# Expert rows gathered four to a token: column-quarter sums for groups of four rows in a ring of eight

## The chip, the core and the metric

The kernel runs on one core of one Trainium2 chip. The metric is device time in microseconds (us) of one execution. PE is TensorE, DVE VectorE, ACT ScalarE, POOL GpSimd, SP the queue that issues the weight transfers. Everything is float32; a float32 matmul stands in the trace as two MATMUL instructions and two weight loads, so "x8" is four matmuls.

## The reference, cut to what matters

Two transformer-like blocks over 256 tokens of 1024 numbers. The change is in one layer of the first block, a mixture of 16384 tiny experts of which each token uses 128:

```python
def peer(h, w_query, sub_keys, expert_u, expert_v):
    ...                                  # two top-16 searches for each of 8 heads
    eidx = ...                           # (tokens, 128) expert numbers
    gate = softmax(top_s)                # (tokens, 128)
    u = expert_u[et]                     # a row of 1024 for every token and expert
    v = expert_v[et]
    act = gelu(einsum('tnd,td->tn', u, xt)) * gt
    return einsum('tn,tnd->td', act, v)
```

Beside it stands work that does not depend on it: the second block's scan over 256 context tokens (projections, a solve by doubling in 64x64 pieces, a chain of states) and a small projection.

## The kernel before

The tokens are two blocks (b = 0, 1) of 128, one token to a partition. `u` and `v` lie side by side in `experts`, so one gather (`pool_rows`, line 1187) fetches 128 rows of 2048 numbers, 1 MB: row i of a tile is the i-th expert of each of the 128 tokens. There are 256 gathers, into a ring of `RING = 9` slots, three groups of `GROUP = 3`. POOL issues a gather into a slot once the slot's former row was used.

For each group, in order: DVE multiplies each row's `u` half with the tokens in `normed` and sums (`dve_group`, line 1197), ACT takes the gelu (1213), DVE multiplies by the gate (1201), ACT builds a 128x128 diagonal matrix of the results for each row (1219), and PE multiplies it with the `v` half, 2 x 512 columns, and so adds up all rows in PSUM (`pe_group`, 1231). From group 26 on (`WIDE`) the third row of each group does not go to PE: DVE adds it to `xres` (1208). At the end of a block `dve_rows_out` (1264) adds the PSUM sums to `xres`.

The order of everything around it is written out by hand in `run_order` (2185). A "turn" is one group; after each group every engine does the next "piece" of the work beside it from the list `pieces`: first the expert searches of the seven later quarters (`dve_select`, five pieces for each, spread over 24 turns), then the context block: its norm, 7 pieces of projection (`pe_ctx_in`), 2 of `dve_scan_common`, and for each of two directions 5 pieces of `pe_direction`/`dve_direction` and two pairs of 9 pieces of the solve (`pe_pair`), then 4 pieces of chain and the projection: 85 pieces in 86 turns. PE does piece n after group n, while ACT and DVE do it after group n+1 (`lag`). Every engine's queue is strictly in this order, so a piece that waits holds up the engine's next group. The search of the first quarter (b = 0) runs alone, before the first gather.

`AUX[:, 0:2, :]` (`SUMS`) collects the rows; the searches take their scores from `sc`, copied out of PSUM by ACT in `act_queries`.

## Time and profile before

| | us |
|---|---|
| median of 3 runs | 1682.56 (1682.3 to 1685.46) |
| the profiled execution | 1685.36 |
| its span | 1683.8 |
| PE busy | 1394.0 (83%) |
| DVE busy | 1029.3 (61%) |
| ACT busy | 358.7 (21%) |
| POOL busy | 347.3 (21%) |
| moved by DMA | 406.98 MB, of which 297.35 MB by the software queue of the gathers |

The profile cuts the span into 40 slices of 42.1 us; a digit is the busy share in tenths. The gathers run in slices 8 to 25. PEclk is the clock that the throttle granted TensorE, as a share of 2.4 GHz. "Idle before, releaser" tells what ended an engine's idle time. Times of day below are us from the start of the span.

### The profile page before, as it was taken

Reading aid. Unit: us, or ns where it says so; the run is one execution under the profiler, and the core shown is the slowest. Engines: PE = TensorE matmul, PEld = TensorE weight load, DVE = VectorE, ACT = ScalarE, POOL = GpSimd, SP = SyncE. Lnnn points to the kernel's source line nnn. Section 1 sums busy time; section 2 is a strip of 40 time slices with the busy share of each in tenths; the row PEclk is TensorE's granted clock in tenths of the full one; section 3 lists DMA queues with packets and bytes.
Section 4 is the critical chain, followed back from the end, with each engine's and each line's share of the span. In section 5 each row is a group of like instructions: output and inputs, shape, how many; then the busy total and the mean of one; then the engine's idle time right before and its main releaser. Section 6 shows DMA issues by size and latency. Waiting matters only on the chain.

```text
span 1683.8 us, 24922 instructions
## 1 busy us (share of the span) xinstructions
PE 1394.0 (83%) x10614; PEld 940.2 (56%) x10614; DVE 1029.3 (61%) x2175; ACT 358.7 (21%) x696; POOL 347.3 (21%) x315
## 2 busy tenths in 40 slices
PE   7989898957677797588859897779987878899997
PEld 6468764832233264255525554347877763788843
DVE  2967765539999877868788777421554343355511
ACT  3012400112222322421242121212342210111100
POOL 1000011124344444445545454000000000000000
PEclk9988998979887898899988998789999999899998
DMA  9453387599989999799999999524200021344442
GB/s 373 165 176 116 110 323 259 187 324 420 373 323 383 366 356 407 267 391 416 419 376 365 418 417 415 219 75 150 101 8 3 4 103 50 112 151 154 154 159 83
DMA packets 110735, 406.98 MB, mean 242 GB/s; under 512 B 10376, under 2 KB 35472, under 8 KB 77344
## 3 DMA queue, kind: packets, MB, share of 16 engines
q0 software_dynamic: 44576, 297.35, 44.3%
q1 hardware_dynamic: 62720, 104.36, 18.1%
q10 hardware_dynamic: 3328, 3.68, 1.2%
q8 instruction: 83, 1.36, 0.3%
q14 instruction: 28, 0.23, 0.0%
HBM read 404.30 MB, written 1.07 MB: 241 GB/s over the span
## 4 chain that ended last, share of the span: by engine, by line
PE 58%; DVE 23%; DMA 8%; ACT 5%; issue 4%; POOL 1%; ACTq 0%; DVEq 0%; another core or an unknown queue 0%
PE psum L489 24%; DVE arena L1197 9%; PE psum L499 7%; PE psum L1231 6%; PE psum L1582 6%; DMA arena<-in_experts,arena 6%; PE psum L2038 4%; PE psum L1785 2%; DMA weights<-in_w_in 1%; PE psum L585 1%; DVE arena L1156 1%; DVE arena L1157 1%; DVE arena L1154 1%; PE psum L708 1%; PE psum L1926 1%
## 5 line engine op out<-in xcount | busy, mean ns | idle before, releaser
L1231 PE MATMUL psum<-arena 128*128 128x512 f32 x792 | 405.9, 665 | 142.0 <-ACT arena L1219 141.6
L489 PE MATMUL psum<-actT,weights 128*128 128x256 f32 x1824 | 404.0, 384 | 5.3 <-ACT actT L602 2.3
L1187 POOL DMA_INDIRECT arena<-in_experts,arena x256 | 317.5, 1240 | 437.9 <-PE psum L1231 370.5
L489 PEld LDWEIGHTS psum<-actT,weights 128*128 128x128 f32 x1824 | 351.1, 193 | 57.5 <-ACT actT L602 5.6
L1231 PEld LDWEIGHTS psum<-arena 128*128 128x128 f32 x792 | 161.8, 212 | 348.7 <-issue 200.3
L1197 DVE CUSTOM_DVE_ANT_0 arena<-normed,arena 128x1024 f32<-128x1024 f32 x256 | 304.7, 1223 | 61.1 <-DMA arena<-in_experts,arena 57.0
L1213 ACT ACTIVATE arena<-arena 128x3 f32<-128x3 f32 (+1 forms) x86 | 17.6, 204 | 441.0 <-DVE arena L1197 384.2
L1582 PE MATMUL psum<-arena 64*64 64x64 f32 (+1 forms) x2816 | 84.6, 224 | 17.5 <-DVE arena L1699 7.1
L1582 PEld LDWEIGHTS psum<-arena 64*64 64x64 f32 x2816 | 79.3, 135 | 24.5 <-issue 14.9
L499 PE MATMUL psum<-weights,actT 128*128 128x512 f32 x192 | 83.1, 593 | 2.1 <-DMA weights<-in_w_in 1.0
L944 POOL DMA_DIRECT2D arena<-in_ada_wT x48 | 25.3, 528 | 252.0 <-DVE mod L960 252.0
L1208 DVE SCALAR_TENSOR_TENSOR xres<-arena,xres 128x1024 f32<-128x1024 f32 x58 | 74.5, 1285 | 2.5 <-DVE arena L1201 0.6
L2038 PE MATMUL psum<-weights,arena 128*128 128x512 f32 x176 | 75.7, 593 | 0.0
L1219 ACT ACTIVATE arena<-const,arena 128x128 f32<-128x128 f32 x198 | 67.2, 393 | 19.8 <-DVE arena L1201 18.9
L499 PEld LDWEIGHTS psum<-weights,actT 128*128 128x128 f32 x192 | 36.3, 190 | 47.8 <-issue 44.9
L2082 DVE SCALAR_TENSOR_TENSOR arena<-arena,small 128x256 f32<-128x256 f32 x154 | 61.9, 480 | 0.0
L2038 PEld LDWEIGHTS psum<-weights,arena 128*128 128x128 f32 x176 | 33.5, 190 | 41.6 <-issue 41.5
L1582 PEld LDWEIGHTS psum<-actT,arena 64*64 64x64 f32 x1152 | 38.8, 134 | 17.5 <-issue 17.0
L2080 DVE TENSOR_SCALAR arena<-arena,small 128x256 f32<-128x256 f32 x22 | 6.8, 351 | 67.5 <-ACT arena L2055 67.5
L819 DVE SCALAR_TENSOR_TENSOR arena<-arena,small 128x256 f32<-128x256 f32 x120 | 47.6, 482 | 0.0
L1582 PE MATMUL psum<-actT,arena 64*64 64x64 f32 x1152 | 44.5, 221 | 3.6 <-issue 3.4
L544 ACT ACTIVATE normed<-xres 128x1024 f32<-128x1024 f32 x7 | 7.4, 1056 | 173.3 <-DVE xres L2100 68.3
(347 smaller groups left out, 1537.4 us busy)
## 6 DMA issues: line engine op xcount, KB each, us to landing
weights<-in_w_in SPq DMA_DIRECT2D x18, 2048.0 KB, 8.9
arena<-in_ada_wT POOLq DMA_DIRECT2D x48, 512.0 KB, 5.8
weights<-in_ffn_w_up SPq DMA_DIRECT2D x22, 1024.0 KB, 6.8
weights<-in_ffn_w_down SPq DMA_DIRECT2D x5, 2048.0 KB, 7.9
weights<-in_w_out SPq DMA_DIRECT2D x4, 2048.0 KB, 15.0
weights<-in_w_peer_q SPq DMA_DIRECT2D x4, 2048.0 KB, 8.5
arena<-in_experts,arena POOLq DMA_INDIRECT x256
weights<-in_w_ple_gate SPq DMA_DIRECT2D x2, 2048.0 KB, 8.2
```

What stands on the lines that cost most here:

```text
L489: mm = nc.tensor.matmul(out[:, c * T:(c + 1) * T], w[:, k, c * P:(c + 1) * P], act[:, k, :], start=(k == 0), stop=(k == kc - 1))
L499: mm = nc.tensor.matmul(out[:, b * 512:(b + 1) * 512], act[:, k, b * P:(b + 1) * P], w[:, k, :], start=(k == 0), stop=(k == kc - 1))
L819: st.run(nc.vector.scalar_tensor_tensor(ycv[:, c, :], src, w, ycv[:, c, :], ALU.mult, ALU.add))
L1187: nc.gpsimd.indirect_dma_start(out=rows[:, n % RING, :], out_offset=None, in_=dram["experts"], in_offset=bass.IndirectOffsetOnAxis(ap=eidx ...
L1197: ins = nc.vector.tensor_tensor_reduce(rows[:, pos, 0:D], normed[:, b, :], rows[:, pos, 0:D], 1.0, 0.0, ALU.mult, ALU.add, dots[:, g, j:j ...
L1208: nc.vector.scalar_tensor_tensor(xres[:, b, :], rows[:, pos, D:2 * D], acts[:, g, ON_PE:GROUP], xres[:, b, :], ALU.mult, ALU.add).then_inc ...
L1219: nc.scalar.activation(diag[:, pos, :], K("ident"), ACT.Copy, scale=acts[:, g, j:j + 1]).then_inc(S("diag_ok"), 1)
L1231: mm = nc.tensor.matmul(SUMS[:, i, :], diag[:, pos, :], rows[:, pos, D + 512 * i:D + 512 * (i + 1)], start=first, stop=last, skip_group_ch ...
L1582: mm = nc.tensor.matmul(dst[half[c], g, at + q * n:at + (q + 1) * n], left(g, c, q), right(g, c, q), start=True, stop=True)
L1785: mm = nc.tensor.matmul(out[:, c * T:(c + 1) * T], w[:, k, c * P:(c + 1) * P], actT[:, k, :], start=(k == 0), stop=(k == DC - 1))
L2038: mm = nc.tensor.matmul(aux[2 * b + n], ffT[:, f, b * P:(b + 1) * P], w[:, k, 512 * n:512 * (n + 1)], start=(f == 0), stop=(f == FC - 1))
L2082: st.run(nc.vector.scalar_tensor_tensor(dst, src, w, dst, ALU.mult, ALU.add))
```

## The change

The 128 slots of a gather are dealt differently: a tile holds for 32 tokens (a quarter of the block) four rows each. Of the 32 gathers of one search, number i serves token quarter g = i % 4, and its partition 32 j + m holds expert 8 j + i // 4 of token 32 g + m; so four gathers in a row serve the four token quarters. Bytes and number of gathers are the same. So the dots need the tokens of a quarter on all four partition quarters (`quad_tokens`, written to DRAM and read back four times), and numbers and gates must be moved from the partition of their token to the four quarters: DVE multiplies them by a mask `quad`, PE sums with `ident_q`, DVE copies out of PSUM. The stationary matrix of a row is now 128x32, and its sum goes to 32 partitions of PSUM; the four rows of a group take the four column quarters of the array.

`RING` is 8 and `GROUP` 4: two groups. All rows go to PE; DVE's addition at 1208 and its gate multiplication at 1201 are gone, and ACT multiplies by the gate, one instruction for each row. PE waits for all four matrices of a group. The pieces are cut anew (ten for each search, a search begun every 8 pieces, 119 in all) and taken two to a turn: 60 of the 64 turns have pieces. PE's first projection of the context waits for all searches.

```diff
-RING = 9
-GROUP = 3
+RING = 8
+GROUP = 4
+QUADS, QP = 4, 32
...
+        high = r.take(2 * D).rearrange("p (g n) -> p g n", g=2)
+        quad_tokens = (normed, high)
...
+        SPREAD = {what: PS[:, 2 * (tile_at["ctx_k"] % 2) + i, 0:HEADS * PK] for i, what in enumerate("eg")}
+        FIRST_E = AUX[:, 0, 0:HEADS * PK]
+        def pe_spread(pe, what, turn, dst):
+            pe.wait_ge(S(f"spread_{what}_in"), turn + 1)
+            if turn:
+                pe.wait_ge(S("eidx_ok" if what == "e" else "gates_done"), turn)
...
+            for j in range(QUADS):
+                mm = nc.tensor.matmul(dst[QP * j:QP * (j + 1), :], K("ident_q"), src[:, n * j:n * (j + 1)],
+                                      start=True, stop=True)
+        def act_quad_tokens(act, b, half):
+            for j in range(QUADS):
+                src = normed_rows[b * P:(b + 1) * P].rearrange("(g t) d -> t g d", g=QUADS)
+                act.dma_start(quad_tokens[half][QP * j:QP * (j + 1), :, :], src[:, 2 * half:2 * half + 2, :]).then_inc(
+                    S(f"quad_in{half}"), 16)
         def pe_queries(pe):
...
             for i in range(QUARTERS + 1):
+                if i == QUARTERS - 1:
+                    pe_spread(pe, "e", 0, FIRST_E)
...
+                    if i == QUARTERS - 1:
+                        pe_spread(pe, "g", 0, SPREAD["g"])
+                        pe.wait_ge(S("eidx_ok"), 1)
...
+            act.dma_start(normed_rows.rearrange("(b p) d -> p b d", p=P), normed).then_inc(S("normed_out"), 16)
...
         def dve_group(dve, b, t, g, count):
             for k, pos, n, filled in turn_slots(b, t, g * GROUP, count):
+                half = k % QUADS // 2
+                if isinstance(t, int) and t == 0 and k < QUADS and k % 2 == 0:
+                    dve.wait_ge(S(f"quad_in{half}"), 16 * QUADS * (b + 1))
                 dve.wait_ge(S(f"row{pos}"), filled * 16)
...
-            dve.wait_ge(S("gelu_ok"), t * PER_TURN + (GROUPS * b + g + 1))
-            nc.vector.tensor_tensor(acts[:, g, 0:count], gelu[:, g, 0:count],
-                                    gate[:, b, bass.ds(t * RING + g * GROUP, count)], ALU.mult).then_inc(S("acts_ok"), 1)
-            if count == GROUP and not wide(b, t, g):
...
-                nc.vector.scalar_tensor_tensor(xres[:, b, :], rows[:, pos, D:2 * D], acts[:, g, ON_PE:GROUP],
-                                               xres[:, b, :], ALU.mult, ALU.add).then_inc(S("row_added"), 1)
         def act_group(act, b, t, g, count):
...
+            act.wait_ge(S("gelu_ok"), t * PER_TURN + (GROUPS * b + g + 1))
+            for j in range(count):
+                nc.scalar.activation(acts[:, g, j:j + 1], gelu[:, g, j:j + 1], ACT.Copy,
+                                     scale=gate[:, b, bass.ds(t * RING + (g * GROUP + j), 1)]).then_inc(S("acts_ok"), 1)
             for k, pos, n, filled in turn_slots(b, t, g * GROUP, count):
                 j = k - g * GROUP
...
+                act.wait_ge(S("acts_ok"), rows_ahead(b, t, g) + j + 1)
+                nc.scalar.activation(diag[:, pos, :], K("ident_q"), ACT.Copy,
+                                     scale=acts[:, g, j:j + 1]).then_inc(S("diag_ok"), 1)
+            if b + 1 < TB and isinstance(t, int) and t == TURNS - 1 and g == PER_TURN - 1:
+                for half in range(2):
+                    act_quad_tokens(act, b + 1, half)
         def pe_group(pe, b, t, g, count):
...
+            pe.wait_ge(S("diag_ok"), rows_ahead(b, t, g) + count)
+            for i in range(2):
+                for k, pos, n, filled in turn_slots(b, t, g * GROUP, count):
+                    part = slice(QP * (k % QUADS), QP * (k % QUADS + 1))
...
+                    mm = nc.tensor.matmul(SUMS[part, i, :], diag[:, pos, :], rows[:, pos, D + 512 * i:D + 512 * (i + 1)],
                                           start=first, stop=last, skip_group_check=True)
+                    if i:
+                        mm.then_inc(S("row_used"), 1)
...
         def pe_ctx_in(pe):
+            pe.wait_ge(S("eidx_ok"), QUARTERS * TB)
+            pe.wait_ge(S("gates_done"), QUARTERS * TB)
...
+        pieces = [sum(pieces[i:i + 2], []) for i in range(0, len(pieces), 2)]
```

In `dve_select` the gate's subtraction goes ahead of the two heads' index sums, which become a piece each; behind them stand the mask products, and in the last piece the copies of numbers and gates out of PSUM.

## Rows read from the trace of the kernel before

**Rows 1.** The page's 40 slices: granted clock and DMA share.
```profile
PEclk9988998979887898899988998789999999899998
DMA  9453387599989999799999999524200021344442
```
**Rows 2.** Stretches of the gathers: us, busy of PE, PEld, DVE, ACT, POOL (instructions), PEclk, DMA share, GB/s.
```profile
378.00:590.00 212.00, 151.19 (x289) 61.55 (x288) 195.37 (x701) 53.17 (x123) 87.60 (x73) 0.85 0.93 373
...
650.00:710.00 60.00, 32.58 (x91) 15.49 (x90) 52.56 (x63) 23.30 (x40) 24.32 (x18) 0.80 0.83 330
710.00:850.00 140.00, 123.38 (x1571) 74.16 (x1569) 106.86 (x172) 31.18 (x84) 69.38 (x57) 0.98 0.99 402
850.00:900.00 50.00, 30.52 (x163) 15.80 (x166) 42.18 (x55) 19.68 (x37) 20.39 (x15) 0.76 0.87 345
900.00:1061.00 161.00, 138.22 (x1605) 81.46 (x1597) 124.37 (x207) 32.10 (x91) 74.97 (x62) 0.93 1.00 412
```
**Rows 3.** The page's costliest groups: those of the row loop, and the solve's.
```profile
L1231 PE MATMUL psum<-arena 128*128 128x512 f32 x792 | 405.9, 665 | 142.0 <-ACT arena L1219 141.6
...
L1197 DVE CUSTOM_DVE_ANT_0 arena<-normed,arena 128x1024 f32<-128x1024 f32 x256 | 304.7, 1223 | 61.1 <-DMA arena<-in_experts,arena 57.0
L1213 ACT ACTIVATE arena<-arena 128x3 f32<-128x3 f32 (+1 forms) x86 | 17.6, 204 | 441.0 <-DVE arena L1197 384.2
L1582 PE MATMUL psum<-arena 64*64 64x64 f32 (+1 forms) x2816 | 84.6, 224 | 17.5 <-DVE arena L1699 7.1
...
L1208 DVE SCALAR_TENSOR_TENSOR xres<-arena,xres 128x1024 f32<-128x1024 f32 x58 | 74.5, 1285 | 2.5 <-DVE arena L1201 0.6
...
L1219 ACT ACTIVATE arena<-const,arena 128x128 f32<-128x128 f32 x198 | 67.2, 393 | 19.8 <-DVE arena L1201 18.9
```
**Rows 4.** Timeline of DVE in the solve: start, us, instruction [idle before <-releaser].
```profile
828.73 1.23 DVE L1197 CUSTOM_DVE_ANT_0 arena<-normed,arena 128x1024 f32<-128x1024 f32 x1 [1.26 <-DMA arena<-in_experts,arena]
```
**Rows 5.** Timeline of POOL and DVE: a group's first gather, its first and last dot.
```profile
623.10 1.17 POOL L1187 DMA_INDIRECT arena<-in_experts,arena  x1 [4.54 <-PE psum L1231]
...
631.29 1.23 DVE L1197 CUSTOM_DVE_ANT_0 arena<-normed,arena 128x1024 f32<-128x1024 f32 x1 [0.67 <-DMA arena<-in_experts,arena]
...
636.43 1.23 DVE L1197 CUSTOM_DVE_ANT_0 arena<-normed,arena 128x1024 f32<-128x1024 f32 x1 [1.41 <-DMA arena<-in_experts,arena]
```
**Rows 6.** Timeline of PE: full width, two column halves, four 64x64 tiles, one cold sum.
```profile
314.55 1.95 PE L1029 MATMUL psum<-arena 128*128 128x128 f32 x16
...
185.22 1.58 PE L699 MATMUL psum<-arena 128*64 128x128 f32 x16 [1.68 <-ACT arena L787]
...
715.54 0.92 PE L1582 MATMUL psum<-arena 64*64 64x64 f32 x46
...
830.88 5.40 PE L1231 MATMUL psum<-arena 128*128 128x512 f32 x8 [2.69 <-ACT arena L1219]
```
**Rows 7.** Timeline at the start: first gather, ACT's last load, first reused slot.
```profile
332.26 1.01 POOL L1187 DMA_INDIRECT arena<-in_experts,arena  x1 [35.49 <-DVE arena L1159]
...
361.36 4.21 ACTq L525 DMA_DIRECT2D arena<-in_ctx  x1
...
371.67 0.94 POOL L1187 DMA_INDIRECT arena<-in_experts,arena  x1 [28.35 <-PE psum L1231]
```
**Rows 8.** Timeline of DVE: the first search's first instruction, its last before the gathers.
```profile
316.38 0.88 DVE L1100 MAX8 arena<-arena 128x8 f32<-128x128 f32 x4 [13.00 <-ACT arena L1046]
...
331.80 0.18 DVE L1159 CAST arena<-arena 128x32 uint32<-128x32 f32 x1
```
**Rows 9.** Timelines of PE and DVE in the context block's projection, common part and direction.
```profile
641.10 5.34 PE L1785 MATMUL psum<-actT,weights 128*128 128x256 f32 x24
...
659.45 6.55 DVE L1430 RECIPROCAL actT<-actT 128x1024 f32<-128x1024 f32 x1 [1.71 <-ACT actT L1417]
...
701.16 2.74 PE L1469 MATMUL psum<-const,arena 128*128 128x128 f32 x16 [4.27 <-DVEq L1560]
```
**Rows 10.** Timeline of DVE: the last block's sums are added.
```profile
1081.66 1.22 DVE L1264 TENSOR_TENSOR xres<-xres,psum 128x1024 f32<-128x1024 f32 x1 [14.50 <-PE psum L1231]
```

More of the change, by code:

```diff
@@ L308, in build @@
         gate = r.take(TB * NSEL).rearrange("p (b n) -> p b n", b=TB)
-        dots = r.take(12).rearrange("p (g n) -> p g n", g=3)
-        gelu = r.take(12).rearrange("p (g n) -> p g n", g=3)
-        acts = r.take(12).rearrange("p (g n) -> p g n", g=3)
-        diag = r.take(RING * P).rearrange("p (g n) -> p g n", g=RING)
+        dots, gelu, acts = [r.take(RING).rearrange("p (g n) -> p g n", n=GROUP) for _ in range(3)]
+        diag = r.take(RING * QP).rearrange("p (g n) -> p g n", g=RING)
         rows = r.take(RING * 2 * D).rearrange("p (g n) -> p g n", g=RING)
+        high = r.take(2 * D).rearrange("p (g n) -> p g n", g=2)
+        quad_tokens = (normed, high)
         after_rows = r.at
@@ L341, in build @@
         gsum = r.take(HEADS)
+        spread_e, spread_g = [r.take(HEADS * PK * QUADS) for _ in range(2)]
         assert r.at <= ARENA - 3072
@@ L1110, in dve_select @@
             st.settle()
+            yield
             for g in range(n_s):
@@ L1182, in pool_rows @@
                     g, j = divmod(k, GROUP)
-                    if j == ON_PE and not wide(former[0], t, g):
-                        pool.wait_ge(S("row_added"), dve_added(former[0], t, g) + 1)
-                    else:
-                        pool.wait_ge(S("row_used"), pe_summed(former[0], t, g) + j + 1)
+                    pool.wait_ge(S("row_used"), rows_ahead(former[0], t, g) + j + 1)
                 nc.gpsimd.indirect_dma_start(
@@ L1238, in groups_of_rows @@
                 t, g = divmod(first, PER_TURN)
-                if t == TURNS:
-                    group(eng, b, t, 0, REST)
-                    first += 1
-                elif g or t == 0 or last - first < 2 * PER_TURN:
+                if g or t == 0 or last - first < 2 * PER_TURN:
                     group(eng, b, t, g, GROUP)
@@ L1245, in groups_of_rows @@
                 else:
-                    end = min(last // PER_TURN, TURNS)
-                    assert GROUPS * b + first >= WIDE
+                    end = min(last // PER_TURN, TURNS - 1)
+                    if group is act_group:
+                        eng.wait_ge(S("gates_done"), TB * QUARTERS)
                     with eng.Fori(t, end) as i:
@@ L1421, in dve_scan_common @@
             wait_freed(dve, m.tiles[0])
+            if not m.full:
+                product(dve, "ctx_lora")
             for c in range(RC):
@@ L2146, in build @@
         beside = [select_stage(b, q) for b in range(TB) for q in range(QUARTERS) if b or q]
-        at_select = [[(i, k)] if k != 2 else [(i, 2), (i, 3)]
-                     for i, f in enumerate(beside) for k in range(f["pieces"]) if k != 3]
         n_first = len(beside)
+        pieces = [[] for _ in range(SELECT_EVERY * (n_first - 1) + SELECT_PIECES)]
+        for i, f in enumerate(beside):
+            for k in range(f["pieces"]):
+                pieces[SELECT_EVERY * i + k].append((i, k))
         beside += [dict(act=act_ctx_norm, dve=dve_ctx_norm, pieces=1),
```

110 lines of the change are left out of this document (59 added, 51 removed).

## The prediction

> **What bounds the kernel now.** I read the slices first [rows 1]: from slice 8 to 25 the DMA share stands at 9 nearly throughout, and nowhere else. This is the stretch of the 256 gathers, and the only one that the change touches. Then the stretches [rows 2]. From 710 to 850 and from 900 to 1061 the DMA share is 0.99 and 1.00 at 402 to 412 GB/s, with DVE busy 76% and PE 86 to 88%: the gathers' bytes are the bound. A tile of 1.049 MB takes 2.55 us there, and the dots wait for it [rows 4]. In the searches (378 to 590) DVE is busy 195.37 of 212 us and DMA has 0.93: DVE is the bound, by a little. In 650 to 710 (DMA 0.83, DVE 52.56 of 60 us) and 850 to 900 (0.87, 42.18 of 50) DVE's lumps of the scan are.
>
> So PE's 405.9 us and DVE's 74.5 us in the row loop [rows 3] are mostly beside the transfers. What is to be had is the time in which DMA is not full: by 1 minus its share, 15 us in the searches, 10 in 650 to 710, 7 in 850 to 900, 3 elsewhere; some 35 us, with 12 us more around 372, where the ring has run dry.
>
> **What the change does to each engine.** PE: a group of four rows was 16 instructions of 0.43 us (405.9 us over 792 is 0.51 with the cold ones) one after another, 6.9 us; in four independent columns of four instructions it is 4 x 0.43 plus 0.2 to drain, 1.9 us, or 3.6 us at 1.2 GHz. That columns do run side by side I read from the trace [rows 6]: 16 instructions of 128 columns at full width took 1.95 us, while 16 on two column halves with the same 128 rows took 1.58, and 46 on four 64x64 tiles 0.92 us, 20 ns each, though each is 0.22 us long. The Trainium skill speaks against this (TensorE: Matmul & The Clock Gate, Part 3, What overlaps and what doesn't): weight loads overlap running matmuls only where the row group differs, and here all four columns use all rows. By it 16 loads, at its P/1.2 ns some 27 ns each, would stand bare, 0.4 us a group. The trace does not bear it out: the halves of L699 share their row groups and overlap all the same.
>
> DVE: loses 58 additions, 74.5 us, and 86 gate products of 0.16; gains, for each search, two mask products and two copies, each bounded by 0.18 [rows 8] and 1.0 us below, I take 0.2 to 0.3, so 0.8 a search and 7 us in all. ACT, for a group of four: gelu 0.20, four gate products, four matrices of 128x32. A product is bounded by 0.14 and 0.20 (gelu of 3 numbers [rows 3]), a matrix by 0.20 and 0.34 (67.2 us over 198, at 128 wide); nearer the lower ends as the tiles are small, so 0.2 + 0.7 + 0.85 and 0.2 for waits on itself: 2.0 us, where a row's first matrix was ready after 0.9. POOL: same 256 issues.
>
> **The new limit: a ring of two groups.** A slot's round is: issue of its gather, landing of the whole group, dots, ACT, sums, next issue. With two groups, a turn (four rows) can't be shorter than half a round. Before, there were three groups, and rows were given back one by one. The round's first part I take from a group whose first gather found the queue nearly empty: issued 623.10, first dot 631.29, third 636.43 [rows 5]; 13.3 us for three, with a fourth transfer 15.9. A row was still ahead in that queue, and weights moved beside it, so this is an upper end; the lower is four transfers (10.2) plus half of what the first dot shows beyond its own transfer (5.6), 13.0. I take 14.6. Then last dot 1.2, ACT 2.0, sums, and an estimated 0.3 us until POOL issues.
>
> In the searches PE does nothing but sums (2 to 4 of 10 us), so its clock will be low, as it is near 0.8 in 650 to 710 with PE busy half the time [rows 2]: 3.6 us. Round 21.7, turn 10.8 us against 10.2 of transfer. DVE's turn is below that: four dots 4.8 (304.7 over 256) and, of a search of 15.6 us [rows 8] plus 0.8, on average a quarter, 4.1 with the gate: 9 us, the worst pair near 10.5.
>
> In the solve (17 of the 31 later turns with pieces) the pairing bites. PE takes pieces 2n and 2n+1 before the next group's sums; 2n+1 needs what ACT and DVE make of 2n, and these do it only after the dots of that next group. So the sums come after dots, ACT's group 2.0, its copies 1.0, PE's piece 2.5: 5.7 instead of 2.0 after the dots (the piece: some 80 instructions at 84.6 us over 2816 [rows 3], 0.03 each; the copies: two of 512 columns, an estimate from 0.34 for 128). Round 14.6 + 1.2 + 5.7 + 1.9 + 0.3 = 23.7, turn 11.8 warm; PE idles 4 us in each such turn, and after 2.69 us of idleness 8 sums took 5.40 us instead of 3.6 [rows 6]. I take 11.8.
>
> **The sum**, from the first reused slot on, against the profiled execution:
> - Start. The first indices pass PE once more: +1.2 us on the first gather at 332.26. Eight rows land instead of nine. ACT is held by its loads until 361.36 + 4.21 [rows 7]; both come 2 us later since PE stands in the new mask sums. Then table, gelu, ACT and a cold sum: the first reused slot is issued at 374.3 instead of 371.67. It must wait for other small transfers, as before (DMA share was full there), so the third group's dots end at about 393.4.
> - 27 more turns in the searches at 10.8: 292, so 685.
> - 34 turns at 10.2: 347, so 1032.
> - Context norm: the sums of that group stand behind transposes that wait for the norm, +5. Projection: two pieces of 5.34 [rows 9] and sums, 12.5 us a turn for three turns, +6. Tokens of block 1: ACT issues eight loads, a landing takes up to 8 us (row 5's 8.2), DVE waits, +5. Together 16.
> - Common part and first direction: six pieces of DVE. The stretch 650 to 710 had DVE busy 52.56; without six additions of 1.28 and twenty dots of 1.19 some 21 us are left, with waits on ACT (7.4 us of idleness) 29; before it one more piece of 4.5. In three turns with 14 us of dots that is 48 for 31 of transfer; two slots' slack of 4 gone: +13. In one of them the sums stand behind PE's wait for DVE L1560 (idle 4.27 [rows 9]) and the preparation of 7 us, +7: together 20.
> - Second direction: the same without the common part, +10.
> - Solve: 17 turns, 11.8 instead of 10.2: +27.
> - Chain: two turns, serial between PE and DVE, +3.
> - After the last dot: ACT 2.0, sums 3.6 cold, semaphores: 6.5 to the end of the addition.
>
> 685 + 347 + 16 + 20 + 10 + 27 + 3 + 6.5 = 1114.5. Before, the addition ended at 1081.66 + 1.22 = 1082.9 [rows 10]. So +31.6 us. What follows is unchanged. The profiled execution took 1685.36, which is the upper end of the three runs; laid on the median 1682.56 it gives **1714 us**.
>
> **Rivals.** (1) The transfers stay the bound: ACT and sums are short enough that a round is below 20.4, and DVE, rid of 74.5 us, catches up. Then 61 turns of 10.2 from 393.4 (1016), half of the lumps (30), 6.5: 1052, which is 31 us less: **1652 us**. For it speak DVE's load and the dry ring at 372 that is no worse; against it that a round of 20.4 leaves 4.6 us between the last dot and the next issue even with 14.6 before it, and the pairing in the solve. Chance 0.2. (2) Half-way: searches at 10.4, solve at 10.8: 11 + 17 us less than the forecast, **1686 us**; chance 0.14. (3) The forecast, with everything from 1695 to 1755: 0.56. (4) The columns don't run side by side with 512 columns moving: 6.9 us warm or up to 13.8 cold for the sums, at least 5 more in a round, 2.5 in each of 61 turns: +150, **1865 us**. Against it [rows 6]; 0.04. By the skill's rule on weight loads alone it would be 0.4 a round, +12: 1726, inside the forecast. (5) Lumps and cold clock are worse (solve at 13.5, searches at 11.3: +29 + 14): 1757 and more, 0.06.
>
> The forecast and (1) part at a round of 20.4 us, in the searches and in the solve.
>
> Range for 8 in 10: down into rival (1), 1655, up to 1757. A measurement of this kernel can tell 0.2%, 3.4 us: faster than 1679.2 has rival (1) and a part of (2), 0.25; within, 0.06; slower the rest, 0.69.
>
> **What would show it.** PE's line of the sums: 1024 instructions with busy time near 110 to 220 us, not 440 or more (rival 4). DVE 70 us less busy. In the searches DMA share near 0.94 with DVE's dots idle before DMA, and POOL idle before PE; a group's turn 10.8 us. In the solve turns of 11.8 and a DMA share of 0.87; at 1.00 rival (1) is right. PEclk lower than now in slices 9 to 16. The last addition near 1114. Wrong I'd be above all if a group's landing is much shorter than 14.6 us once the queue runs empty each time, or if the new waits on ACT's own results cost more than 0.2.

## The result, and the profile of the changed kernel

The changed kernel takes 1800.41 us (median of 4 runs, 1797.06 to 1811.26), the kernel before 1682.52 beside it: 1.0707 times as long, 95% interval 1.0660 to 1.0755. That is +118 us. The forecast was +31.6 us and 1714, with a range up to 1757, which is 43 us below the result. So the direction was right and the size was not, by nearly a factor of four.

The 40 slices of the changed kernel's page, granted clock and DMA share, to be laid beside [rows 1] (a slice is 45.0 us here and 42.1 there; both count from 0):
```profile
PEclk9979998955656555876786778759999998899999
DMA  9444496999999999776887698952420002355432
```
Slices 9 to 15 look no worse than before in DMA share, a 9 throughout; the loss is plain to see only from slice 16 on. This first impression is wrong, as the stretches show (us, busy time of PE, PEld, DVE, ACT and POOL with their instructions, PEclk, DMA share, GB/s), cut at the ends of the groups 2, 29, 33, 37, 46, 49 and 58 of four rows:
```profile
392.00:699.00 307.00, 98.03 (x544) 19.02 (x544) 239.77 (x775) 71.15 (x265) 128.82 (x108) 0.58 0.96 369
699.00:765.00 66.00, 36.90 (x178) 23.67 (x179) 24.22 (x41) 15.47 (x47) 13.54 (x14) 0.71 0.83 280
765.00:839.00 74.00, 30.44 (x164) 18.84 (x162) 45.48 (x53) 27.16 (x65) 20.56 (x19) 0.70 0.64 244
839.00:956.00 117.00, 80.83 (x1552) 61.02 (x1552) 55.84 (x94) 31.25 (x106) 45.48 (x38) 0.79 0.84 327
956.00:1007.00 51.00, 19.99 (x184) 11.21 (x184) 31.29 (x41) 21.57 (x51) 14.11 (x11) 0.64 0.61 231
1007.00:1122.00 115.00, 78.58 (x1460) 57.72 (x1456) 56.37 (x94) 30.77 (x106) 41.83 (x37) 0.82 0.85 329
1122.00:1202.00 80.00, 34.18 (x240) 13.37 (x240) 32.20 (x61) 13.34 (x56) 19.74 (x19) 0.66 0.84 336
```
In the first stretch, the searches, the share is 0.96 and yet only 369 GB/s are moved. Before, 0.99 and 1.00 went with 402 to 412 GB/s [rows 2]. A DMA engine that is "busy" here moves less than it did there. The searches of before, where VectorE was the bound, moved no more, 373 GB/s at 0.93 [rows 2]. So in this stretch nothing is lost against before; what is missing is the gain that the relieved VectorE should have brought. The last dot of the 120th row ends at 698.7 us, before at 711.0, though before had by then done the context's projection and the common part [rows 9], and the changed kernel neither. The loss of the whole falls behind that row. In the two solve stretches (839 to 956, 1007 to 1122) the share is 0.84 and 0.85, where 0.87 was forecast and before had 0.99 and 1.00; PE is busy 69% of them and DVE 48%, so nothing in them is full.

The costliest groups of the row loop and the solve on the page, beside [rows 3] (busy us, mean ns of one | idle time of the engine just before them and what ended most of it):
```profile
L1275 PE MATMUL psum<-arena 128*32 128x512 f32 x1024 | 192.0, 890 | 313.7 <-ACT arena L1262 313.7
L1233 POOL DMA_INDIRECT arena<-in_experts,arena x256 | 299.2, 1169 | 573.8 <-PE psum L1275 476.1
...
L1246 DVE CUSTOM_DVE_ANT_0 arena<-arena 128x1024 f32<-128x1024 f32 x128 | 155.4, 1224 | 116.5 <-DMA arena<-in_experts,arena 106.5
L1246 DVE CUSTOM_DVE_ANT_0 arena<-normed,arena 128x1024 f32<-128x1024 f32 x128 | 153.2, 1223 | 70.3 <-DMA arena<-in_experts,arena 57.8
L1252 ACT ACTIVATE arena<-arena 128x4 f32<-128x4 f32 x64 | 13.1, 205 | 528.2 <-DVE arena L1246 510.0
L1626 PE MATMUL psum<-arena 64*64 64x64 f32 (+1 forms) x2816 | 87.1, 230 | 23.1 <-DVE arena L1743 7.1
...
L1262 ACT ACTIVATE arena<-const,arena 128x32 f32<-128x32 f32 x256 | 60.2, 305 | 0.0
...
L1257 ACT ACTIVATE arena<-arena 128x1 f32<-128x1 f32 x256 | 54.4, 283 | 5.9
```
The change does to the engines what it says. The sums keep PE busy for 192.0 us instead of 405.9, although each single instruction is longer (890 ns against 665): four run at a time. The additions on DVE are gone (DVE is busy 950.5 us, before 1029.3). But the dots now wait 106.5 + 57.8 = 164 us for gathers, before 57.0, and POOL waits 476 us for the sums that free its slots, before 370.5. Two engines were relieved that were not the bound, and the bound, the transfers, is fed late.

One round of a slot in the searches, out of the timeline of POOL, DVE, ACT and PE (start, us, instruction [idle before <-releaser]): group 17 from its first gather to the gather that takes its first slot again.
```profile
545.27 1.62 POOL L1233 DMA_INDIRECT arena<-in_experts,arena  x1 [3.93 <-PE psum L1275]
...
549.88 0.94 POOL L1233 DMA_INDIRECT arena<-in_experts,arena  x1 [0.31 <-issue]
...
560.96 1.22 DVE L1246 CUSTOM_DVE_ANT_0 arena<-arena 128x1024 f32<-128x1024 f32 x1 [1.26 <-DMA arena<-in_experts,arena]
562.22 0.20 ACT L1252 ACTIVATE arena<-arena 128x4 f32<-128x4 f32 x1 [8.94 <-DVE arena L1246]
562.52 0.85 ACT L1257 ACTIVATE arena<-arena 128x1 f32<-128x1 f32 x4
563.28 0.94 ACT L1262 ACTIVATE arena<-const,arena 128x32 f32<-128x32 f32 x4
564.27 3.64 PE L1275 MATMUL psum<-arena 128*32 128x512 f32 x16 [7.59 <-ACT arena L1262]
568.16 0.94 POOL L1233 DMA_INDIRECT arena<-in_experts,arena  x1 [5.17 <-PE psum L1275]
```
From 545.27 to 562.18, the end of the last dot, are 16.9 us; ACT takes 2.0, the sums 3.6, and 0.25 later the slot is issued again: 22.9 us. Over the 25 groups from 4 to 28 the means are 16.7, 2.0, 3.6 and 0.3, a round of 22.7 and a turn of 11.4. The forecast was 15.8, 2.0, 3.6, 0.3 and 10.8.

One turn of the solve, with a pair of pieces, from the timeline of all engines:
```profile
1068.75 1.21 DVE L1246 CUSTOM_DVE_ANT_0 arena<-arena 128x1024 f32<-128x1024 f32 x1
...
1070.00 0.20 ACT L1252 ACTIVATE arena<-arena 128x4 f32<-128x4 f32 x1 [8.47 <-DVE arena L1246]
1070.30 0.85 ACT L1257 ACTIVATE arena<-arena 128x1 f32<-128x1 f32 x4
1071.05 0.94 ACT L1262 ACTIVATE arena<-const,arena 128x32 f32<-128x32 f32 x4
...
1072.84 0.58 ACT L1711 COPY arena<-psum 128x512 f32<-128x512 f32 x1
1073.47 1.97 PE L1626 MATMUL psum<-actT,arena 64*64 64x64 f32 x32 [3.44 <-ACT arena L1711]
1075.23 1.92 PE L1626 MATMUL psum<-arena,actT 64*64 64x64 f32 x32
...
1076.94 1.69 PE L1626 MATMUL psum<-actT,arena 64*64 64x64 f32 x32
1078.56 1.92 PE L1275 MATMUL psum<-arena 128*32 128x512 f32 x16
1078.71 0.69 DVE L1743 TENSOR_TENSOR actT<-actT,psum 128x512 f32<-128x512 f32 x1 [8.75 <-PE psum L1626]
```
The matrices are ready at 1071.99, and the sums start at 1078.56, 6.6 us later. Between them stands TensorE's second piece, which itself waited 3.44 us for ACT's copies, and these had stood behind the dots. Behind it DVE has waited 8.75 us, with the next dots queued after it. This is the pairing as the prediction described it. The forecast for this gap was 3.7 us. The turn shown (group 54) has the longest of the second solve; the mean over groups 50 to 58 is 4.4 us.

### The profile page after: what moved, and what is told of

Its sections match the earlier page's. It is cut to its first block and busy times, and to the rows that moved or that the text cites. A ratio compares the mean times of both kernels' runs of the same rounds, so it can differ in the third digit from the quotient of the medians.

```text
span 1800.5 us, 25862 instructions
## 1 busy us (share of the span) xinstructions
PE 1218.2 (68%) x10974; PEld 843.9 (47%) x10974; DVE 950.5 (53%) x2055; ACT 395.8 (22%) x987; POOL 329.0 (18%) x315
## 3 DMA queue, kind: packets, MB, share of 16 engines
q1 hardware_dynamic: 62720, 104.38, 16.9%
## 5 line engine op out<-in xcount | busy, mean ns | idle before, releaser
L1275 PE MATMUL psum<-arena 128*32 128x512 f32 x1024 | 192.0, 890 | 313.7 <-ACT arena L1262 313.7
L1233 POOL DMA_INDIRECT arena<-in_experts,arena x256 | 299.2, 1169 | 573.8 <-PE psum L1275 476.1
L493 PEld LDWEIGHTS psum<-actT,weights 128*128 128x128 f32 x1824 | 350.9, 193 | 57.8 <-ACT actT L606 5.6
L1275 PEld LDWEIGHTS psum<-arena 128*32 128x32 f32 x1024 | 34.6, 143 | 432.6 <-ACT arena L1262 323.7
L1246 DVE CUSTOM_DVE_ANT_0 arena<-arena 128x1024 f32<-128x1024 f32 x128 | 155.4, 1224 | 116.5 <-DMA arena<-in_experts,arena 106.5
L1246 DVE CUSTOM_DVE_ANT_0 arena<-normed,arena 128x1024 f32<-128x1024 f32 x128 | 153.2, 1223 | 70.3 <-DMA arena<-in_experts,arena 57.8
L2128 DVE SCALAR_TENSOR_TENSOR arena<-arena,small 128x256 f32<-128x256 f32 x154 | 61.9, 478 | 0.0
L1262 ACT ACTIVATE arena<-const,arena 128x32 f32<-128x32 f32 x256 | 60.2, 305 | 0.0
L1626 PE MATMUL psum<-arena,actT 64*64 64x64 f32 (+1 forms) x896 | 44.7, 258 | 20.0 <-DVE actT L1743 7.9
L1257 ACT ACTIVATE arena<-arena 128x1 f32<-128x1 f32 x256 | 54.4, 283 | 5.9
L1626 PEld LDWEIGHTS psum<-arena,actT 64*64 64x64 f32 x896 | 40.2, 160 | 28.3 <-DVE actT L1743 8.2
```

The costliest lines, as they stand in the source:

```text
L493: mm = nc.tensor.matmul(out[:, c * T:(c + 1) * T], w[:, k, c * P:(c + 1) * P], act[:, k, :], start=(k == 0), stop=(k == kc - 1))
L1233: nc.gpsimd.indirect_dma_start(out=rows[:, n % RING, :], out_offset=None, in_=dram["experts"], in_offset=bass.IndirectOffsetOnAxis(ap=eidx ...
L1246: ins = nc.vector.tensor_tensor_reduce(rows[:, pos, 0:D], quad_tokens[half][:, j % 2, :], rows[:, pos, 0:D], 1.0, 0.0, ALU.mult, ALU.add, ...
L1257: nc.scalar.activation(acts[:, g, j:j + 1], gelu[:, g, j:j + 1], ACT.Copy, scale=gate[:, b, bass.ds(t * RING + (g * GROUP + j), 1)]).then_ ...
L1262: nc.scalar.activation(diag[:, pos, :], K("ident_q"), ACT.Copy, scale=acts[:, g, j:j + 1]).then_inc(S("diag_ok"), 1)
L1275: mm = nc.tensor.matmul(SUMS[part, i, :], diag[:, pos, :], rows[:, pos, D + 512 * i:D + 512 * (i + 1)], start=first, stop=last, skip_group ...
```

## The experiments

Ratios are against the kernel before, run beside on the same chip; the medians of before were 1683.13, 1682.47, 1681.63 and 1682.26 us. The theory to be tested had two parts: a ring of two groups that feeds the transfers late, and pairs of pieces that hold up sums and dots.

**A ring of two groups in the old layout.** The kernel before with one constant changed, so six slots in two groups of three:
```diff
-RING = 9
+RING = 6
```


> The kernel before with a ring of six slots, two groups of three, and nothing else changed. Theory A (a ring of two groups is a round that can't be shorter than issue, landing, dots, matrices and sums, and a turn is half of it): in the changed kernel a group of four took 16.5 us from its first issue to the end of its last dot; with three rows about 13.5, plus 2.6 until the first row is summed and 0.3 to the issue, so 16.4 a round and 8.2 a turn instead of 7.55 where the transfers bind, +40 us, and another 7 to 10 us at each of three lumps of DVE: 1725 to 1750. Theory B (the loss comes from pairs of pieces and from the new waits, not from the depth of the ring): within 10 us of 1683.

Measured 1789.99 us, 1.0640 [1.0598, 1.0683]. This ring, with groups of three, one piece a turn, additions on DVE and full-width sums, costs +107 us, more than the 42 to 67 that I gave it. The stretch from 395 to 650, in the kernel before and in this run:
```profile
395.00:650.00 255.00, 197.62 (x481) 97.19 (x482) 220.85 (x716) 61.50 (x146) 106.84 (x86) 0.87 0.94 368
```
```profile
395.00:650.00 255.00, 177.03 (x380) 80.03 (x379) 203.07 (x683) 54.62 (x129) 92.61 (x78) 0.82 0.83 321
```
DMA share 0.83 and 321 GB/s instead of 0.94 and 368: two groups of three don't keep the queue filled. The edit changes two things at once: there are two groups instead of three, and six rows instead of nine. So it shows what this ring costs, not which of the two does it.

**The new layout without both suspects.** Groups of two, so four groups in the ring of eight and one piece at each of 128 turns:
```diff
-GROUP = 4
+GROUP = 2
-        assert TURNS * RING == NSEL and RING % QUADS == 0 and GROUP == QUADS
+        assert TURNS * RING == NSEL and RING % QUADS == 0
-        pieces = [sum(pieces[i:i + 2], []) for i in range(0, len(pieces), 2)]
```


> The changed kernel with groups of two rows in the same eight slots, so four groups, and one piece a turn instead of two (128 turns, 119 pieces). Same gathers, same narrow sums, but only two column quarters at a time. Theory A: a round is divided by four, 15 us over 4 is below the 5.1 us that two rows take to transfer, so the transfers bind again: 248 rows of 2.55 to 2.6 us from 379 on, 20 us of lumps, 15 for the reload of the tokens, 10 for the end, gives 1670 to 1700. Theory B: the same if pairs are the cause. Theory C (the rows of four tokens' quarters are slower to fetch, 3.0 us instead of 2.55, whatever the ring): 1780 or more.

Measured 1702.22 us, 1.0122 [1.0091, 1.0153], 2 us above what theories A and B gave; theory C is out. So of the 118 us, 98 belong to the groups of four and what came with them, and 20 to the rest. The searches:
```profile
392.00:664.00 272.00, 154.61 (x542) 28.73 (x538) 233.27 (x730) 78.21 (x286) 130.16 (x107) 0.74 1.01 417
```
417 GB/s, four rows in 10.2 us. The 32-wide matrices and the tokens spread over the partitions are not what slows the searches. The run can't tell groups of four from pairs, since it takes both away; the next ones do.

**Pairs alone.** The same, with two pieces at every second turn and none at the others:
```diff
+        pieces = [p for i in range(0, len(pieces), 2) for p in (sum(pieces[i:i + 2], []), [])]
```


> As the kernel with groups of two, but two pieces at every second turn and none between, which is the changed kernel's rhythm of two pieces in four rows. Theory A: the ring of four groups gives back most, pairs cost a few us at lumps and in the solve where sums stand behind two pieces: 1700 to 1730. Theory B (pairs are the cause): near 1780 to 1800.

Measured 1780.39 us, 1.0583 [1.0544, 1.0623], the number of theory B: pairs alone cost 78 us, though the ring holds four groups. In the searches they cost nothing (the 120th row's dot ends at 665.8 us, without pairs at 664.1). In the solves (groups 38 to 45 and 50 to 57) four rows take 14.3 and 14.7 us instead of 10.6 and 11.0. DVE's timeline there, one pair:
```profile
1057.53 0.69 DVE L1743 TENSOR_TENSOR actT<-actT,psum 128x512 f32<-128x512 f32 x1 [6.46 <-PE psum L1626]
1060.40 0.69 DVE L1743 TENSOR_TENSOR actT<-actT,psum 128x512 f32<-128x512 f32 x1 [2.19 <-PE psum L1626]
1061.01 1.22 DVE L1246 CUSTOM_DVE_ANT_0 arena<-normed,arena 128x1024 f32<-128x1024 f32 x1
```
DVE waits for PE with the rows' dots behind it, and these were not late: it is no wait for a gather.

**The tokens of block 1.** The changed kernel without its second load of tokens; block 1 is computed with the tokens of block 0, and nothing else is left out:
```diff
-                    dve.wait_ge(S(f"quad_in{half}"), 16 * QUADS * (b + 1))
+                    dve.wait_ge(S(f"quad_in{half}"), 16 * QUADS)
-            if b + 1 < TB and isinstance(t, int) and t == TURNS - 1 and g == PER_TURN - 1:
-                for half in range(2):
-                    act_quad_tokens(act, b + 1, half)
```


> The changed kernel without the second block's load of the tokens: block 1 is computed with the tokens of block 0 (this part of the computation is changed). In the trace DVE is idle 6.5 and 10.1 us before dots that wait for this load, and a turn there takes 32 us. If the load is what it waits for: 15 to 20 us less, 1780 to 1785. If the second context projection on PE (10.6 us a pair) would bind there anyway: 5 us less or nothing.

Measured 1791.51 us, 1.0649 [1.0610, 1.0689], 9 us less than the change, where I expected 15 to 20. In the changed kernel DVE shows 16.6 us of waits for these loads:
```profile
736.72 1.22 DVE L1306 TENSOR_TENSOR xres<-xres,psum 128x1024 f32<-128x1024 f32 x1 [9.74 <-PE psum L1275]
744.47 1.22 DVE L1246 CUSTOM_DVE_ANT_0 arena<-normed,arena 128x1024 f32<-128x1024 f32 x1 [6.53 <-DMA normed<-normed_rows]
...
756.90 1.23 DVE L1246 CUSTOM_DVE_ANT_0 arena<-arena 128x1024 f32<-128x1024 f32 x1 [10.05 <-DMA arena<-normed_rows]
```
Without the loads the turn of group 32 is 15.2 us instead of 32.3, but that of group 33 10.9 instead of 5.6: rows that had landed behind the wait have to be waited for now. The prediction had put 5 us for it.

**Pairs only in the searches.** The changed kernel, with single pieces from the context's norm on; the 29 that no longer find a turn run after the last row:
```diff
-        pieces = [sum(pieces[i:i + 2], []) for i in range(0, len(pieces), 2)]
+        n_search = SELECT_EVERY * (n_first - 1) + SELECT_PIECES
+        pieces = [sum(pieces[i:i + 2], []) for i in range(0, n_search, 2)] + [[], []] + pieces[n_search:]
...
+                for late in pieces[n_groups - lag:]:
...
```


> The change's kernel with the pieces paired during the searches alone; from the context's projection on there is one piece at each turn again, and the 29 pieces for which the rows then have no turns left run after the last row. So its whole time is not the question (estimate 1770 to 1850 us, a span of rows that ends earlier and a stretch of scan without rows behind it); the turns of groups 38 to 58 are. With the change's own kernel they take 12.9 us. Theory R (a ring of two groups alone holds the turn, pairs only fill it): they stay at 12.0 or above. Theory P (the two pieces of a turn hold the sums back and the ring cannot catch up): they fall to 10.2 to 11.3, the searches' turns (11.35) staying as they are.

Measured 1839.09 us in one run, which is not the question here. The searches are as before the edit (11.4 us a turn). The nine turns 50 to 58 take 11.1 us, in the changed kernel 12.8. In this run the solve fills turns 47 to 63, at 11.4 us on average. The turns 38 to 58 that I had named take 11.7 us on average, in the changed kernel 13.5, both with the lumps of the common part and the directions among them. So theory R, 12.0 or above, is out, and P's 10.2 to 11.3 is met in the nine turns and missed by 0.1 over all of the solve: the pair holds the turn. But without it the turn is not the 10.2 us of full transfers either. It falls to the ring's own, which is near that of the searches. What DVE waited for in 955 to 1055 (total us, times, longest), the view's only row:
```profile
DVE arena L1246 <- DMA arena<-in_experts,arena: 49.9, 37, 3.8
```
and in the changed kernel's solve, 1007 to 1122:
```profile
DVE actT L1743 <- PE psum L1626: 30.8, 7, 8.7
DVE arena L1246 <- DMA arena<-in_experts,arena: 13.2, 11, 2.7
```

**How many gathers are ahead.** The groups of two, ring of eight as it was, but each gather also waits until an earlier row has been used, so that at most 6, or 4, are ahead:
```diff
-                if n >= RING:
-                    former = divmod(n - RING, NSEL)
+                if n >= DEPTH:
+                    former = divmod(n - DEPTH, NSEL)
```


> The groups of two with their ring of 8 rows, but each gather waits until row n-6 (not n-8) has been used, so that at most 6 gathers are ahead. Nothing else is changed. Theory D (a transfer slows when few gathers are queued, whatever the size of the groups): the searches' turns, 5.1 us for two rows, go to 5.5 to 6.2, at a packet time above 325 ns, and the whole to 1740 to 1800. Theory G (what costs is that four rows are given back at once): turns stay at 5.1 to 5.3 and the whole within 15 us of 1702.

> As the kernel before it, with 4 gathers ahead: two groups of two rows. The round of a group is then issue 2.2, the wait for the data 2, transfer 5.1 or more, semaphore 2.7, dots 2.4, ScalarE 1.2 and sums 1.9 to 3.6, some 18 to 19 us for two groups, so 9 to 9.5 us a turn in place of 5.1, and the searches' 29 us for three of them. Over 128 turns that is +500 us: 2150 to 2230. With theory D the transfer grows as well, to 6 us a group, and adds little, since the queue stands empty anyway.

"Ahead" means issued and not yet used. Measured 1735.42 us (1.0322 [1.0273, 1.0370]) with 6, and 2010.40 us (1.1957 [1.1900, 1.2014]) with 4. The searches, first with 6, then with 4 ahead:
```profile
392.00:697.00 305.00, 159.92 (x544) 29.78 (x544) 236.85 (x744) 79.29 (x292) 127.69 (x109) 0.74 0.97 372
```
```profile
402.00:828.00 426.00, 186.84 (x544) 32.64 (x544) 237.41 (x747) 79.31 (x291) 121.03 (x109) 0.61 0.73 266
```
This is the finding on the searches. With 6 ahead and 4 at the lowest, the groups of two take 305 us for 27 times four rows; the changed kernel, with 8 ahead and 4 at the lowest, takes 306. The DMA rows of the two agree as well, 0.97 at 372 GB/s and 0.96 at 369. The whole came out 5 us below the lowest that I expected of theory D, the searches' turn (5.65 us for two rows) inside. With 4 ahead I expected 9 to 9.5 us a turn, 2150 us at least, and saw 7.9 and 2010. Taken apart (means of groups 8 to 57), the round is 15.8 us: 2.1 from the issue to the first data, 6.9 of data, 0.5 to the last dot, 1.2 for it, 1.2 for ScalarE, 3.4 for the sums, 0.3 to the issue. I had put 4.2 for the first, 2.7 for the third and 2.4 for the dots, of which one runs while data still come in. The transfer I had put too low: it takes 6.9 us, not 5.1 or 6.

Counted by the landed packets instead, on average 3.5 gathers are issued and not fully landed in the groups of two (420 to 650 us), 2.7 with 6 ahead, 1.7 with 4, and 2.9 in the changed kernel. This count takes the packets in the order of their start, as the trace doesn't name their gather.

**Rows given back by four, pieces one at a time.** The groups of two once more, only that TensorE sums all four rows at every second group:
```diff
+            if g % 2 == 0:
+                return
             pe.wait_ge(S("diag_ok"), rows_ahead(b, t, g) + count)
             for i in range(2):
-                for k, pos, n, filled in turn_slots(b, t, g * GROUP, count):
+                for k, pos, n, filled in turn_slots(b, t, (g - 1) * GROUP, 2 * count):
```


> The groups of two (1702 us), where TensorE takes no sums at even groups and all sixteen of four rows at odd ones, so rows come back in fours as in the change, while dots, ScalarE's part and the beside pieces (one a turn) stay by two. At least 4 gathers are ahead, as in the change and in the run that was held to 6. Theory D (what counts is how few gathers are ahead at the lowest): four rows take 11.2 to 11.5 us in the searches (the change 11.35, the groups of two 10.2), which is +27 to +35 there, the solves, bound by their pieces at 10.9 us for four rows, go to 11.1 to 11.5, and the whole comes to 1738 to 1760; what is left to the change's 1800 is then the price of the pairs in the change's own ring. If pairs cost there nothing, it comes to 1790 or above; if only the pairs cost, it stays within 10 of 1702.

Measured 1735.34 us, 1.0309 [1.0279, 1.0339]. Searches and second solve:
```profile
394.00:690.00 296.00, 98.06 (x544) 19.48 (x544) 236.23 (x749) 79.31 (x291) 134.49 (x108) 0.59 0.98 381
...
956.00:1053.00 97.00, 66.33 (x1386) 44.85 (x1380) 58.81 (x102) 30.89 (x113) 41.40 (x36) 0.88 0.97 390
```
The sums cost PE the same 98 us as in the change and PEclk is as low, 0.59 against 0.58. Rows given back by four cost 33 us over the groups of two, 3 less than the lowest I expected. Of these, 21 are in the searches, where I expected 27 to 35: four rows take 11.0 us, in the changed kernel 11.4; probably because dots and matrices of the first two rows are through when the last ones land, which no run shows by itself. The solve's nine turns take 10.7 us for four rows, in the changed kernel 12.8. The remaining 65 us to the change's 1800 are not all pairs. Some 11 of them are in the searches (306 us against 296), where pairs cost nothing in the run before; they go with dots and matrices by four. Some 55 lie behind the searches, and those I put down to the pairs in the changed kernel's ring. That ring with single pieces throughout was not run: its 64 turns don't hold the 119 pieces.

**The pair cut differently.** The changed kernel; TensorE alone takes at turn t the second piece of pair t-1 and the first of pair t:
```diff
-        pieces = [sum(pieces[i:i + 2], []) for i in range(0, len(pieces), 2)]
+        flat = pieces + [[]] * (len(pieces) % 2)
+        pieces = [flat[i] + flat[i + 1] for i in range(0, len(flat), 2)]
+        pe_pieces = [flat[0]] + [flat[i - 1] + flat[i] for i in range(2, len(flat), 2)] + [flat[-1]]
```


> The change's kernel (groups of four, ring of two, 1800 us) with its pairs of pieces cut differently on TensorE alone: at turn t it takes the second piece of pair t-1 and the first of pair t, where the other engines keep their pairs. Theory S (a pair costs since TensorE's second piece waits for ScalarE's and VectorE's first, which stand behind the next group's dots, so that the next sums come behind both): the solves' turns fall from 12.9 us to 11.3 to 11.8, the ring's own round as in the searches, and the whole by 34 to 50 us, to 1745 to 1768. Theory W (a pair costs since twice the work stands in a turn, in whatever order): within 10 us of 1800. The searches' turns stay at 11.35 by both.

Measured 1814.40 us, 1.0764 [1.0732, 1.0795]: no gain. It is 14 us above the changed kernel, but the two intervals overlap. Theory S has fallen, and W's number, within 10 us of 1800, was missed by 4. What was waited for in the solves (1012 to 1132), DVE first, then PE:
```profile
DVE actT L1743 <- PE psum L1626: 40.8, 6, 9.3
```
```profile
PE psum L1275 <- ACT arena L1262: 37.6, 8, 5.5
```
The sums do come 0.1 us after their matrices, as meant. But now the loop closes the other way: the second piece on TensorE stands behind the sums, the sums behind the dots, and DVE's second piece, with the next dots behind it, waits for the second piece on TensorE. A turn takes 13.4 us. The sums, which now follow idleness of up to 5.5 us, are slower too (144 instructions 30.7 us, in the changed kernel's solve 21.0). So the price of a pair isn't only the place of the sums in PE's queue. By the waits of both kernels, two pieces in one turn make a chain PE, ACT and DVE, PE, DVE within that turn, and the rows' own chain, dots, ACT, sums, runs through the same queues. Whoever is put first, one stands in the other.

**Lumps.** The groups of two with three edits: the context's projection in pieces of 8 instead of 12 matmuls (10 pieces instead of 7), the ple projection in four pieces instead of one, and each half of block 1's tokens loaded behind its own last user; the cores of the first two:
```diff
-                        if n % 12 == 0:
+                        if n % 8 == 0:
...
-            for i in range(2):
-                pe_tokens(pe, f"ple_proj{i}", pT)
-            yield
+            for i in range(2):
+                w, out = pe_tile(pe, f"ple_proj{i}")
+                kc = w.shape[1]
+                for b in range(TB):
+                    ...
+                    yield
```


> The groups of two (1702 us) with three edits: the context's projection in pieces of 8 matmuls instead of 12, the ple projection in four pieces instead of one, and each half of block 1's tokens loaded right behind its last user. If what is left of the change's loss there is lumps of TensorE (the sums of group 119 wait 17 us behind the ple projection, those of group 63 wait 13 us behind the context's) it gives 1677 to 1690. If the loss sits in VectorE's lumps of the common part and the directions (turns of 13 to 18 us around group 70) it stays at 1695 to 1702.

Measured 1676.69 us, 0.9966 [0.9947, 0.9986]: at the lower end of what the lumps should give, 25 us less than without the edits, and 0.3% below the kernel before. The three edits were not run apart. One wait remained near the end, 10.40 us in front of the first quarter of the projection, with the sums behind it:
```profile
1041.15 3.75 PE L1357 MATMUL psum<-weights,arena 128*128 128x512 f32 x4 [10.40 <-issue]
```
The profile names no releaser, but the loads of the projection's weights and tokens are issued at 1029.88 us, and the later one lands at 1041.06, just before. In the next kernel there are two empty turns between that load and its user, and the common part's reciprocal stands in a turn of its own; the context's projection goes in pieces of 9 matmuls:
```diff
+            yield
+            yield
...
             st.link(nc.vector.reciprocal(m.e, m.e))
+            yield
             st.link(nc.vector.tensor_tensor(m.kk, m.kk, m.e, ALU.mult))
```


> The groups of two with spread pieces (1676.7 us) with two edits more: two empty turns between the load for the ple projection and its first quarter, for which TensorE's queue stood 10.4 us and the sums of group 122 11.0 us, and the common part's reciprocal (6.6 us of VectorE) apart from the product behind it, in a turn of its own; the context's projection goes in pieces of 9 matmuls to make room. If each lump costs what the ring can't cover: 5 to 10 us for the first, 0 to 5 for the second, 1662 to 1672. If the transfers are behind anyway by what the lumps around group 73 took: 1674 to 1680.

Measured 1666.23 us, 0.9902 [0.9882, 0.9922]. The first quarter of the projection no longer waits:
```profile
1043.60 2.52 PE L1361 MATMUL psum<-weights,arena 128*128 128x512 f32 x4
```
The time is won there (from the 236th row's dot to the last one's 53 us instead of 60), not at the common part (66.4 and 65.8 us for its 16 rows). This is the fastest kernel of the study: the change's own layout, in groups of two, with the work beside it spread. The old layout was not given the same spreading, so the 1.0% below before is the price of layout and schedule together, not of the layout; like for like, with the lumps as they were, the layout in groups of two stood at +1.2%.

## Why the prediction was wrong

**What held.** Sums in four quarters run side by side: 16 instructions in 1.92 us warm and 3.64 cold, the 1.9 and 3.6 of the sum. By the rule of the Trainium skill (TensorE: Matmul & The Clock Gate, Part 3, What overlaps and what doesn't) weight loads of columns that share their rows would stand bare, 0.4 us a group. The trace does not agree: 1.92 us is what the sum gave without them. ACT's chain is 2.0 us, as put. Group 2's dots end at 392.3 us (forecast 393.4), the tail is 7.1 (6.5). The two places of loss, a ring of two and the pairs, are the ones that the sum named.

**The step that failed first: the landing.** I put it at 14.6 us for four rows, from one group that came into a nearly empty queue, and called its 15.9 an upper end. It is 15.5 (16.7 less the last dot): 2.6 to the first data, 12.3 of data, 0.6 to the last dot. My 14.6 rested on a transfer of 10.2 us for four rows that was taken from the full queue [rows 2, 4]; the data of four rows flow for 10.4 us in the groups of two, and for 12.3 in the changed kernel. The runs with 8 and 6 ahead show what it hangs on, with layout and group size held: 2.55 against 2.82 us a row. Turn 11.4 instead of 10.8: +15 us in the searches (306 for the forecast 292).

**The second step: the pair.** From the last dot to the end of the sums I put 7.6 us: 5.7, whose three terms add up to 5.5 only, and 1.9 for warm sums. It is 8.9 on average in groups 38 to 45 and 50 to 58; in the latter 6.4 until the sums and 2.5 for them, since not all are warm. With the landing of 15.5 that is a turn of 12.8 to 13.0, not 11.8: +22 us in the 18 turns, of which the sum had 17 at 11.8 and one at 10.2. The landing's share in it is nearly half. For the other turns after the searches the sum used 10.2 us, the full transfers; by its own terms the ring's turn with warm sums was 10.0, ((15.8 + 2.0 + 1.9 + 0.3) / 2). With the landing as measured it is 10.5 warm and 11.3 cold, so 10.2 could not be kept up.

**The third, and the largest with 51 us: lumps.** I priced them as if the ring had slack for two slots and each lump were met once. Over their forecasts came the projection and tokens +9 us (66.2 for groups 30 to 33), common part and first direction +13 (73.8), second direction +10 (50.7), and the end +19 (73.4). Of the end the sum had nothing but the chain's 3 us; the ple projection was put at nothing, without a reason. TensorE stood 9.77 us before the ple projection and then worked on it for 9.06, the sums of group 60 behind it:
```profile
1139.39 3.64 PE L1275 MATMUL psum<-arena 128*32 128x512 f32 x16
1152.80 9.06 PE L503 MATMUL psum<-weights,arena 128*128 128x512 f32 x16 [9.77 <-issue]
1161.80 1.92 PE L1275 MATMUL psum<-arena 128*32 128x512 f32 x16
```
The last addition starts at 1201.3 us and ends at 1202.5, not 1114.5, so +119.6 against [rows 10]. 15 + 22 + 9 + 13 + 10 + 19 less 1 at the start is 87 of the 88 us that were missing; the rest is the tail. These lumps are neither pairs nor groups of four alone: with groups of two and single pieces the common part and first direction take 73.7 us as well, the end 65.7. Spreading the pieces there brought 25 us, and the rests before the ple projection with the separate reciprocal 10 more.

**The rivals.** (1) and (2) are out: a round of 20.4 us was never reached. (4) is out by the sums' busy time. (5) was the case that came, at the chance of 0.06, and its price, +43, covered half: I had put the searches at 11.3, which is what they took, and the solve at 13.5, above the 12.9 that came, but had left lumps and end as they were.

**How the 118 us part.** By the runs in this order: new layout in groups of two +20, rows given back by four +33, and +65 for what is left, of which some 55 are the pairs in that ring and some 11 dots and matrices by four in the searches. In another order, pairs +78, then groups of four on top +20: 32 us more in the searches (306 against 274) and 28 less in groups 38 to 58 (284 against 312). So pairs cost less in groups of four than in groups of two; why, no run shows. Giving back by four and pairs, each taken alone, make 33 + 78 = 111, more than the 98 that both cost together with dots and matrices by four. That the old layout pays +107 for its ring of two is a third number; its sums are full width and hold slots longer, and it has six rows where the new one has eight, but no run here took that apart.

What stays open: why a gather's packets take longer with fewer gathers ahead. In the searches the mean of the gathers' packets of 8 KB is 316 ns with 8 ahead, 339 with 6, 357 with 4, and 339 in the changed kernel. The trace gives each packet's time, not what it waits for.

## What to carry to other kernels

When a ring is cut into fewer, larger groups, what counts is the number of transfers still ahead at the moment before a group is given back; take the transfer's duration from a row where that number is as low, not from the full queue. Avoid two dependent pieces of side work in one turn of a pipelined loop that runs through the same engines: at equal work per row it cost here some 55 to 78 us, and changing the order on one engine only changed who waited. List every piece of side work in the sum, the last one too: the lumps were the largest miss here. Before judging a layout by one kernel, run it with its group size and its schedule undone: here +7.1% became +1.2% in groups of two, and -1.0% once the work beside it was spread, which the old layout might gain from as well.

## What the runs showed of the hardware that was not expected

- The DMA share is no measure of throughput here: 0.96 at 369 GB/s in the changed kernel's searches, 0.97 at 372 with 6 gathers ahead, 1.01 at 417 with 8. The share fell by 4 to 5 points where the rate fell by 11 to 12%.
- Per gather of 1.049 MB in the searches: 2.55 us with 8 ahead given back by two, 2.74 given back by four, 2.82 with 6 ahead, 3.95 with 4 ahead. From the start of a group's first gather on POOL to its first data 2.1 us pass when the queue is nearly empty (4 ahead), and 0.5 us from its last data to the last dot. Four gathers of the changed kernel flow for 12.3 us, 341 GB/s, with the neighbours' data among them. The Trainium skill (DMA: Bandwidth & Descriptors, Anatomy of one DMA — SWDGE (gpsimd) path) fits one DMA on this path as 2.0 us, setup and completion together, plus its bytes over 436 GB/s. By that fit four gathers of 1.049 MB behind one start take an estimated 11.6 us; with 4 to 8 ahead the trace shows 15.5 from the issue to the last dot.
- Four quarters of the array's columns, all on the same 128 rows with 512 columns moving, take 3.64 us for 16 instructions at the low clock and 1.92 at the high one. The granted clock of the searches was 0.58 where sums took 98 us of 307 in bursts by four, and 0.74 where they came by two and took 155 us of 272.
